# A decoder layer on one core: the down projection by seven products in place of eight

## What is computed

```python
h = rmsnorm(x, norm_ffn_g)
gate, new_ffn = causal_dwconv(h @ w_gate, ffn_prev, conv_ffn_w, conv_ffn_b)
x = x + (jax.nn.silu(gate) * (h @ w_up)) @ w_down
```

## Time and profile before

| | us |
|---|---|
| median of 3 runs | 2380.34 |
| lowest, highest | 2379.96, 2383.45 |
| the profiled execution | 2380.18 |
| its span | 2378.6 |
| TensorE busy in the span | 2334.8 |
| VectorE, ScalarE, POOL busy | 1328.9, 806.6, 255.0 |

### The profile page before, as it was taken

One profiled execution on the slowest core, in us unless ns is written; L12 is line 12 of the kernel. 1 busy time (PEld: TensorE's weight loads), 2 busy tenths in 40 slices (PEclk: granted clock), 3 DMA queues, 4 the chain that ended last, 5 costly groups with the idle time before them and its releaser, 6 DMA issues.

```text
span 2378.6 us, 42862 instructions
## 1 busy us (share of the span) xinstructions
PE 2334.8 (98%) x17506; PEld 2324.2 (98%) x17506; DVE 1328.9 (56%) x1653; ACT 806.6 (34%) x1033; POOL 255.0 (11%) x355
## 2 busy tenths in 40 slices
PE   8999999999999899999999999999999999999996
PEld 7999999999999899999999999999999999999996
DVE  6357654456322857877877877877873322222332
ACT  6224322123111434444444444444442111111222
POOL 2210000000322000111111111111111000000111
PEclk9999999999999999999999999999999999999998
DMA  7322232324433234344344344344358543342222
GB/s 246 100 73 73 72 89 72 88 71 152 128 99 111 79 99 127 103 136 125 101 136 122 104 136 119 107 136 116 110 170 281 169 144 125 123 155 91 80 76 85
DMA packets 360893, 281.09 MB, mean 118 GB/s; under 512 B 8168, under 2 KB 348259, under 8 KB 355552
## 3 DMA queue, kind: packets, MB, share of 16 engines
q1 hardware_dynamic: 346960, 203.98, 29.6%
q0 software_dynamic: 13840, 75.76, 8.7%
HBM read 238.86 MB, written 40.85 MB: 118 GB/s over the span
## 4 chain that ended last, share of the span: by engine, by line
PE 97%; DVE 1%; DMA 1%; ACT 0%; issue 0%; POOL 0%; POOLq 0%; SPq 0%; DVEq 0%; ACTq 0%
PE ps L1539 19%; PE ps L1541 19%; PE ps L1540 19%; PE ps L1823 13%; PE ps L1825 12%; PE ps L1824 12%; DMA raw<-in_w_down_dram 0%; PE ps L1677 0%; PE ps L1909 0%; PE ps L1690 0%; DVE h_lo L1052 0%; DMA x_nat<-in_x_prompt_dram 0%; PE ps L1689 0%; PE ps L1597 0%; PE ps L1669 0%
## 5 line engine op out<-in xcount | busy, mean ns | idle before, releaser
L1539 PE MATMUL ps<-h_hi,w_hi 128*128 128x288 f32 x1792 | 531.6, 297 | 2.2 <-issue 2.0
L1026 DVE TENSOR_TENSOR w_lo<-raw,w_hi 128x1024 fp32r<-128x1024 f32 x216 | 270.4, 1269 | 470.0 <-ACT w_hi L636 262.1
L1541 PE MATMUL ps<-h_hi,w_lo 128*128 128x288 f32 x1792 | 527.9, 295 | 0.0
L1540 PE MATMUL ps<-h_lo,w_hi 128*128 128x288 f32 x1792 | 527.8, 295 | 0.0
L1539 PE MATMUL ps<-acts,w_hi 128*128 128x288 f32 x1408 | 415.5, 295 | 0.1
L1541 PE MATMUL ps<-acts,w_lo 128*128 128x288 f32 x1408 | 415.4, 295 | 0.0
L1540 PE MATMUL ps<-acts,w_hi 128*128 128x288 f32 x1408 | 414.6, 294 | 0.0
L1539 PEld LDWEIGHTS ps<-h_hi,w_hi 128*128 128x128 f32 x1792 | 336.4, 188 | 3.5 <-issue 2.7
L1540 PEld LDWEIGHTS ps<-h_lo,w_hi 128*128 128x128 f32 x1792 | 336.5, 188 | 0.0
L1541 PEld LDWEIGHTS ps<-h_hi,w_lo 128*128 128x128 f32 x1792 | 336.3, 188 | 0.0
L1823 PE MATMUL ps<-hq,w_hi 128*128 128x288 f32 x960 | 283.9, 296 | 0.0
(11 more groups left out here) (261 smaller groups left out, 4185.3 us busy)
## 6 DMA issues: line engine op xcount, KB each, us to landing
raw<-in_w_gate_dram SPq DMA_DIRECT2D x88, 512.0 KB, 4.7
raw<-in_w_down_dram SPq DMA_DIRECT2D x88, 512.0 KB, 3.6
raw<-in_w_in_dram SPq DMA_DIRECT2D x80, 512.0 KB, 4.4
act_scratch<-stage POOLq DMA_DIRECT2D x44, 576.0 KB, 3.1
acts<-act_scratch POOLq DMA_DIRECT2D x18, 1152.0 KB, 5.6
raw_c<-in_w_up_dram SPq DMA_DIRECT2D x40, 512.0 KB, 6.6
raw_d<-in_w_up_dram SPq DMA_DIRECT2D x40, 512.0 KB, 5.2
raw<-in_w_out_dram SPq DMA_DIRECT2D x32, 512.0 KB, 3.9
```

Source lines behind the costliest of these rows:

```text
L1026: v.tensor_tensor(w_lo[:, c % 4], raw[:, c % 2], w_hi[:, c % 4].bitcast(F32), ALU.subtract).then_inc(lo_ready, 1)
L1539: te.matmul(out, whi, xhi, start=start, stop=False)
L1540: te.matmul(out, whi, xlo, start=False, stop=False)
L1541: return te.matmul(out, wlo, xhi, start=False, stop=stop)
```

## The change

The down projection too is made by one level of Strassen's scheme. Inner tiles are taken in 22 pairs and output tiles in 8 pairs, columns in two halves; 7 products of the pairs replace 8. The 22 pairs come in six chunks of 3, 3, 4, 4, 4 and 4, each with 8 visits, one for a pair of output tiles: 48 visits of 7 products, and a product has 3 matmuls for each pair of its chunk.

- The activations are now stored as seven forms: four are differences that VectorE makes once per pair of tiles (`act_t1`, `act_t32`, `act_t4`), each with its high and low part. They go out in four stores a pair, rounds 0 to 3 of 576, 576, 576 and 288 KB: round 0 with the even tile, 1 to 3 with the odd one; round 2 has a buffer of its own (`stage_b`). u_gelu becomes `ue`, five halves, and `up_sum` shares two of them, so ScalarE's copy of a PSUM half into up_sum waits, in every even quad, for the low part of round 1 (`act_ready`).
- SP loads one piece of w_down a visit, of 768 KB (3 pairs) or 1 MB (4 pairs), in two buffers. POOL makes two sums of weight blocks per visit (`sums13`), VectorE two (`down_s2`, `down_s4`). ScalarE and VectorE split each of the 7 weight forms, 384 or 512 columns.
- ScalarE copies three partial sums of a visit out of PSUM (`bank_snap`), POOL adds them to X (`snap_add`), and VectorE adds the four banks, one of them to two places (`add_c`, `add_b`, `sub_d`, `add_a`).
- Twelve places hold the forms of the activations; the next chunk's come in while a chunk runs, the last two of its seven only in the last visit before it.
- At the border POOL issues the loads of the first seven forms, the first weight sums, and then, once the last product of gate/up is done, the first quarter of x2. The last pair's rounds 2 and 3 are made and stored in visits 1 and 3.
- In the last chunk three of the four banks rotate, and the transposes stand between the products.

The core of the diff (VectorE's and POOL's part of a visit, and TensorE's):

```diff
+            def sums13(v):
+
+                pool.wait_ge(down_landed[v % 2], 16 * (v // 2 + 1))
+                if v == 1:
+                    pool.wait_ge(piece_done, D0)
+                g.tensor_tensor(down_sum(v), down_form(v, 6), down_form(v, 5), ALU.add).then_inc(s13_ready, 1)
+                g.tensor_tensor(down_form(v, 6), down_form(v, 0), down_form(v, 6), ALU.subtract).then_inc(s13_ready, 1)
...
+            sums13(0)
+            rows_ffn(FT - 1)
             pool.wait_ge(piece_done, D0)
             load_x(0)
...
+                snap_add(v, 0, p1_snap, 2 * gv, 0)
+                if v > LAST_V:
+                    fin_sum(2 * gv - 2)
+                snap_add(v, 1, p5_snap, 2 * gv + 1, 1)
+                if v + 1 < VISITS * len(CHUNKS):
+                    sums13(v + 1)
+                if v > LAST_V:
+                    fin_sum(2 * gv - 1)
+                snap_add(v, 2, u2_snap, 2 * gv, 1)
...
+            NV = VISITS * len(CHUNKS)
+            for vi in range(NV):
+                gv, m = vi % VISITS, NQ * vi
+                j = 2 * gv
+                if vi >= 1:
+                    add_a(vi - 1, 2 * ((vi - 1) % VISITS))
+                    down_lo(m + 3)
+                down_lo(m + 4)
+                if vi > LAST_V:
+                    out_store(j - 2, 0)
+                down_lo(m + 5)
+                if vi < VISITS and gv % 2 == 0:
+                    dve.wait_ge(x_back[gv // 2], 16)
+                add_c(vi, j)
+                down_lo(m + 6)
+                if vi + 1 < NV:
+                    down_lo(m + 7)
+                    down_s2(vi + 1)
+                if vi > LAST_V:
+                    out_store(j - 1, 1)
+                add_b(vi, j)
+                if vi + 1 < NV:
+                    down_lo(m + 8)
+                sub_d(vi, j)
+                if vi + 1 < NV:
+                    down_lo(m + 9)
+                    down_s4(vi + 1)
...
+            def down_product(vi, k, bank, start, stop):
+
+                m = NQ * vi + k
+                n = visit(vi)[1]
+                form = NQ * (vi // VISITS) + k
+                pe.wait_ge(lo_ready, D0 + m + 1)
+                if vi % VISITS == 0:
+                    pe.wait_ge(form_landed[form % 12], 16 * (form // 12 + 1))
```

More of the change, by code:

```diff
@@ L223, in build_layer @@
         act_stored = sem("act_stored")
-        acts_landed = [sem(f"acts_landed{i}") for i in range(5)]
         x_back = [sem(f"x_back{i}") for i in range(4)]
@@ L944, in quad @@
                 form_hi(i, u, 6)
-                if prev:
-                    act_hi_out(q - 1)
+                act_hi(j, 0 if u % 2 else 2, first=not prev)
                 act.wait_ge(piece_done, n + 4)
@@ L1485, in _ @@
[L1485 to L1496 removed]
+            down_lo(2)
@@ L1869, in states_t @@
                              ident[:, :]).then_inc(rows_t, 1)
-            def down_piece(m, t, bank, buf, f, start, stop):
-                c = (D0 + m) % 4
-                for half in range(2):
-                    cols = slice(half * HALF, (half + 1) * HALF)
-                    for k in range(4):
-                        last = three(ps[:, bank + half, 0:HALF], w_hi[:, c, 2 * k + t, :], w_lo[:, c, 2 * k + t, :],
-                                     acts[buf][:, f + k, 0, cols], acts[buf][:, f + k, 1, cols],
-                                     start and k == 0, stop and k == 3)
-                return last
```

597 lines of the change are left out of this document (403 added, 194 removed).

## The result

The changed kernel takes 2410.9 us (median; 2408.8 to 2413.4), the kernel before 2380.2: ratio 1.0126, 95% interval 1.0109 to 1.0144, 30.7 us slower. The forecast was 2395, +15, within 2345 to 2435: the direction and the range held, the size was half of what came.

The account below looks back on a forecast made before the run. The prediction took TensorE to bound the kernel: 2380.2 - 70.4 (528 fewer matmuls) + 25 (3-pair visits) + 2 (4-pair visits) + 26 (last chunk) + 12 (border) + 20 (gate/up) = 2395 us, range 2345 to 2435.

## What to carry to other kernels

Where a wait is carried from turn to turn, price it by what is late in a turn beyond what that turn wins back, not against the margin of one turn. Here a store's bytes were cheap behind a burst of loads and dear inside it: look at the next waited-for landing before placing a DMA issue. Prices on a path that two engines share hold only for the pairs of operations that really share it; look in the trace for one of each kind beside the other engine. Add gains from a reference that was measured more than once, and count them by the stage that was edited.
